# Router logits computed before the token rows are transposed, and a new order of expert steps in the first layer

## What is computed

```python
s = sigmoid(t @ w_router)                 # t: (tokens, 1024), 16 experts
sel = s + b_router
# best of 4 groups by the sum of its top 2, then the top 2 experts inside it
wts = wts / sum(wts)
for e in range(16):
    y = (silu(t @ w_gate[e]) * (t @ w_up[e])) @ w_down[e]     # 1024 -> 512 -> 1024
    out = out + combine[:, e:e + 1] * y
```

## Time and profile before

| | |
|---|---|
| median of 3 runs | 1533.33 us (1530.64 to 1534.82) |
| the profiled execution | 1535.0 us, span 1533.2 us |
| PE busy | 1305.8 us, 85% |
| DVE busy | 606.1 us, 40% |
| ACT busy | 411.2 us, 27% |
| DMA | 381.25 MB, mean 249 GB/s |
| mean granted clock of TensorE | 0.911 |

### The profile page before, as it was taken

One profiled execution on the slowest core, in us unless ns is written; L12 is line 12 of the kernel. 1 busy time (PEld: TensorE's weight loads), 2 busy tenths in 40 slices (PEclk: granted clock), 3 DMA queues, 4 the chain that ended last, 5 costly groups with the idle time before them and its releaser, 6 DMA issues.

```text
span 1533.2 us, 19883 instructions
## 1 busy us (share of the span) xinstructions
PE 1305.8 (85%) x8082; PEld 819.7 (53%) x8082; DVE 606.1 (40%) x1069; ACT 411.2 (27%) x643; POOL 117.0 (8%) x111
## 2 busy tenths in 40 slices
PE   3889999899999799899989836998799858778873
PEld 1477777687777353234333335876688634222321
DVE  0445567676462621111121145557767351101112
ACT  1432236462341400010000026336556300000000
POOL 0000000000040020000000020009702010000001
PEclk9889999999999869899999957999999959979986
DMA  9676753222220599869997953763334469999995
GB/s 385 250 285 247 288 224 150 72 77 76 90 84 6 218 347 385 328 243 366 367 390 265 374 210 140 317 258 138 115 133 141 190 264 330 393 408 387 402 422 180
DMA packets 63951, 381.25 MB, mean 249 GB/s; under 512 B 9552, under 2 KB 14356, under 8 KB 24436
## 3 DMA queue, kind: packets, MB, share of 16 engines
q1 hardware_dynamic: 45056, 338.71, 56.6%
q10 hardware_dynamic: 14708, 24.36, 4.8%
q0 software_dynamic: 4096, 16.91, 3.1%
HBM read 358.71 MB, written 42.21 MB: 261 GB/s over the span
## 4 chain that ended last, share of the span: by engine, by line
issue 42%; PE 37%; DVE 8%; ACT 5%; DMA 5%; POOL 3%; ACTq 0%; POOLq 0%; DVEq 0%; SPq 0%
PE bank L1734 9%; PE bank L1735 8%; PE bank L1736 8%; PE bank L1742 2%; POOL m_lo L645 2%; DMA hrow_d<-in_hy_bias 1%; PE bank L1700 1%; ACT L679 1%; DMA raw<-in_mod 1%; DMA stage<-in_in 1%; POOL x_rows L659 1%; DMA yg<-y_rows,rowid 1%; PE bank L1999 1%; PE bank L1750 1%; DVE wlo L1099 1%
## 5 line engine op out<-in xcount | busy, mean ns | idle before, releaser
L2085 PE MATMUL bank<-wexp,xg 128*64 128x512 f32 (+1 forms) x1504 | 294.6, 646 | 60.0 <-DMA wexp<-in_expert 57.0
L1734 PE MATMUL bank<-h_hi,whi 128*128 128x512 f32 (+1 forms) x640 | 227.8, 356 | 6.8 <-DVE h_lo L1099 5.7
L1735 PE MATMUL bank<-h_lo,whi 128*128 128x512 f32 (+1 forms) x640 | 221.3, 346 | 0.0
L1736 PE MATMUL bank<-h_hi,wlo 128*128 128x512 f32 (+1 forms) x640 | 220.8, 345 | 0.0
L2085 PEld LDWEIGHTS bank<-wexp,xg 128*64 128x64 f32 (+1 forms) x1504 | 79.2, 131 | 237.1 <-issue 160.4
L1099 DVE TENSOR_TENSOR wlo<-stage,whi 128x2048 fp32r<-128x2048 f32 x56 | 132.0, 2365 | 66.2 <-ACT whi L679 53.5
L2100 PE MATMUL bank<-wexp,act_a 128*32 128x256 f32 (+1 forms) x1072 | 146.0, 497 | 6.8 <-DVE act_a L1099 6.5
L679 ACT ACTIVATE yrow<-bank 128x512 f32<-128x512 f32 (+1 forms) x47 | 23.8, 506 | 435.7 <-PE bank L2100 346.2
L1734 PEld LDWEIGHTS bank<-h_hi,whi 128*128 128x128 f32 x640 | 125.3, 196 | 27.8 <-DVE h_lo L1099 7.9
L1735 PEld LDWEIGHTS bank<-h_lo,whi 128*128 128x128 f32 x640 | 125.5, 196 | 13.4 <-issue 0.5
L1736 PEld LDWEIGHTS bank<-h_hi,wlo 128*128 128x128 f32 x640 | 125.3, 196 | 13.7
(11 more groups left out here) (282 smaller groups left out, 1703.0 us busy)
## 6 DMA issues: line engine op xcount, KB each, us to landing
wexp<-in_expert SPq DMA_DIRECT2D x192, 1024.0 KB, 16.3
stage<-in_in SPq DMA_DIRECT2D x40, 1024.0 KB, 4.9
stage<-in_mod SPq DMA_DIRECT2D x26, 1024.0 KB, 7.2
spare<-in_mod SPq DMA_DIRECT2D x14, 1024.0 KB, 18.3
x_rows<-in_c_zero SPq DMA_DIRECT2D x20, 512.0 KB, 7.3
y_rows<-in_c_zero SPq DMA_DIRECT2D x20, 512.0 KB, 8.8
stage<-in_out SPq DMA_DIRECT2D x8, 1024.0 KB, 4.8
raw<-in_mod SPq DMA_DIRECT2D x8, 1024.0 KB, 7.1
```

The lines of the kernel that those rows point to most:

```text
L1734: MM(o, w[0], x_[0], start=start, stop=False)
L1735: MM(o, w[0], x_[1], start=False, stop=False)
L1736: return MM(o, w[1], x_[0], start=False, stop=stop)
L2085: ins = MM(bank[0][g * w:(g + 1) * w, :], x_[:, 2 * j + k, :], wexp[:, z, j, c], start=(first_ == 0), stop=(last_ == 0))
```

## The change

In both layers TensorE now makes all eight logit products first; only then come the transposes of the row banks, b = 0 first, then those of the logits, then the other banks. ScalarE loads the sigmoid's table before it makes h2T, makes all h2T tiles in one run, and copies all row banks but the last two after the sigmoid; VectorE copies the last two after its masks. Of the eight lead units two stand before "places" and six after. In layer 0 the order of ranks is another: ranks 5, 7, 4, 8, 3 and 11 come first, and the four steps of ranks 1, 0 and 2 are parted by steps of ranks 10, 12, 14, 9, 13 and 6. Capacities, layer 1's order and all arithmetic are the same.

```diff
-ORDER = ((3, 3, 4, 4, 1, 11, 1, 1, 1, 0, 10, 0, 14, 0, 13, 0, 7, 5, 5, 12, 2, 2, 6, 2, 2, 8, 9),
+ORDER = ((5, 5, 7, 4, 4, 8, 3, 3, 11, 1, 1, 10, 1, 12, 1, 0, 0, 14, 0, 9, 0, 2, 2, 13, 2, 6, 2),
          (0, 7, 9, 5, 3, 3, 14, 4, 11, 2, 2, 13, 8, 1, 1, 12, 6, 10))
...
                 pool.wait_ge(S("rowid_ok"), 1)
-                pool.wait_ge(S("row_a"), T // P)
-                pool.wait_ge(S("row_d"), T // P)
+                pool.wait_ge(S("row_a"), 2 * (T // P) - 2)
+                pool.wait_ge(S("row_d"), 2)
...
+                nc.scalar.preload_act_table(ACT.Sigmoid)
                 for k in range(KT):
                     act.wait_ge(S("hn"), (KT if l == 0 else 2 * KT) + k + 1)
...
-                    if 4 <= k < 4 + NT and k % 2 == 0:
-                        rows_out_(k - 4)
 
                 act.wait_ge(S("lg"), 1)
                 fn(lgT[:, 0:T], bank[7][0:NE, 0:T], ACT.Copy).then_inc(S("lgT"), 1)
-                rows_out_(NT)
                 act.wait_ge(S("lg"), 2)
                 fn(rt[:, 0, 0:NT * NE], bank[7][:, 0:NT * NE], ACT.Sigmoid).then_inc(S("affin"), 1)
-                for b in range(NT + 2, 2 * NT, 2):
+                for b in range(2 * NT - 2):
                     rows_out_(b)
...
-                for b in range(1, NT, 2):
-                    rows_out_(b)
...
                 ins.then_inc(S("routed"), 1)
-                for b in range(NT + 1, 2 * NT, 2):
+                for b in range(2 * NT - 2, 2 * NT):
                     rows_out_(b)
...
                     ins = MM(bank[7][0:NE, 0:T], wr[:, k, :], h2T[:, k, 0:T], start=(k == 0), stop=(k == KT - 1))
-                    if k < 4:
-                        for t in range(NT):
-                            row = T_(row_bank(t)[:, k * P:(k + 1) * P], h2T[:, k, t * P:(t + 1) * P])
-                            if k == 3:
-                                row.then_inc(S("rows"), 1)
                 ins.then_inc(S("lg"), 1)
-                for t in range(NT):
-                    if NT + t >= 7:
-
-                        pe.wait_ge(S("row_a"), 1)
+                for b in range(2 * NT):
+                    if b >= 7:
+
+                        pe.wait_ge(S("row_a"), b - 6)
                     for k in range(4):
...
                 if l < DEPTH - 1:
-                    pe.wait_ge(S("row_a"), 3)
-                    pe.wait_ge(S("row_d"), 2)
-                    lead_units(0, LEAD // 2)
+                    pe.wait_ge(S("row_a"), LEAD_BANK + 1)
+                    lead_units(0, 2)
                 pe.wait_ge(S("routed"), 1)
...
                 if l < DEPTH - 1:
-                    lead_units(LEAD // 2, LEAD)
-                pe.wait_ge(S("row_a"), NT)
-                pe.wait_ge(S("row_d"), NT)
+                    lead_units(2, LEAD)
+                pe.wait_ge(S("row_a"), 2 * NT - 2)
+                pe.wait_ge(S("row_d"), 2)
```

More of the change, by code:

```diff
@@ L1999, in _ @@
                     ins = MM(bank[7][0:NE, 0:T], wr[:, k, :], h2T[:, k, 0:T], start=(k == 0), stop=(k == KT - 1))
-                    if k < 4:
-                        for t in range(NT):
-                            row = T_(row_bank(t)[:, k * P:(k + 1) * P], h2T[:, k, t * P:(t + 1) * P])
-                            if k == 3:
-                                row.then_inc(S("rows"), 1)
                 ins.then_inc(S("lg"), 1)
-                for t in range(NT):
-                    if NT + t >= 7:
-                        pe.wait_ge(S("row_a"), 1)
+                for b in range(2 * NT):
+                    if b >= 7:
+                        pe.wait_ge(S("row_a"), b - 6)
                     for k in range(4):
-                        row = T_(row_bank(NT + t)[:, k * P:(k + 1) * P], h2T[:, 4 + k, t * P:(t + 1) * P])
+                        row = T_(row_bank(b)[:, k * P:(k + 1) * P], h2T[:, 4 * (b // NT) + k, (b % NT) * P:(b % NT + 1) * P])
                     row.then_inc(S("rows"), 1)
-                    if t == 0:
+                    if b == 0:
                         pe.wait_ge(S("lgT"), 1)
```

## The result

The changed kernel took 1517.26 us (median of four runs, 1512.96 to 1518.20), the kernel before 1534.07, measured beside it (four runs, 1530.64 to 1540.98): a ratio of 0.9872, 95% interval 0.9852 to 0.9892, so 16.8 us less. A later comparison gave 0.9895 (0.9865 to 0.9924). The forecast was 8.4 us less, with a range that reached to 1516. The direction held; the size was half of what came.

A forecast was written before the change was run, and what follows sets the result against it. Layer 0's experts were taken as bound by weights for 70 us, then mostly TensorE; layer 1's by weights. Gains of 4.8 (layer 0) and 3.6 (layer 1) sum to 8.4 us: 1533.3 to 1524.9 us, range 1516 to 1532.

The forecast's parts named there:

- What bounds the kernel: Layer 0's expert stage: weights for its first 70 us, then mostly TensorE; layer 1's expert stage: weights alone.
- The dynamic tail behind: End of layer 0's expert stage, one extra item, its weights and row stores: left as it is, no gain.
- Routing, layer 0: Layer 0's sigmoid, and the weight stream after it, come 4.6 us earlier.
- The new order: Layer 0's 27 expert steps under the new rank order end at 867.3 instead of 872.1, 4.8 us earlier.
- The 37th piece: Layer 0's weight stream: rank 1's fourth piece, counted from the restart at 554.9, lands at 674.9 and releases TensorE.
- rival (c): Better than forecast: layer 0's weights come at 3.0 us a piece and tail waits shrink; 1516 us, chance 0.15.
- Rival (a): Layer 0's order gives back the earlier stream's gain, leaving only layer 1's 3.6 us; 1529.7 us, chance 0.14.
- Rival (b): Slower: weight starvation in layer 0's steps 2 to 9 decides, slower overall from 3.42 us a piece; 1542, chance 0.08.
- stretch at half clock: Sign against the mechanism: TensorE running at half clock behind 680 us in layer 0; a 14 us stretch costs 7 us.
- Rival (d): All eight router products run at low clock, layer 0's sigmoid 0.4 us later; 1531.1 us, held in (a)'s chance.
- Routing, layer 1: Layer 1's sigmoid and its weight stream start 3.6 us earlier, all of it kept; bounds 2.4 to 5.3.
- The table load: ScalarE's sigmoid table load leaves the path to the sigmoid in each layer: 1.28 us, no drain counted.

The follow-up runs named there:

- number 3: The changed kernel with only the end of layer 0's order altered, so that single-step rank 9 again comes last in slot 0; 1522.56 us, ratio 0.9910.
- numbers 1: The changed kernel with layer 0's old order of ranks, so only the routing is new; 1526.91 us, ratio 0.9944.
- number 5: New routing and old order, with the six weight pieces of layer 0's extra item cut to 256 columns; 1517.07 us, ratio 0.9886.
- number 4: New routing with the old order's first 19 steps and its end changed to the new order's pattern; 1524.26 us, ratio 0.9933.
- number 11: The changed kernel itself, unaltered, measured once more; 1516.06 us, ratio 0.9895.
- number 7: The changed kernel without the sigmoid's table load ahead of the h2T pieces; 1516.47 us, ratio 0.9860.

## Why the prediction was right in direction and half in size

**What bounds the kernel** was read rightly for the steps and for layer 1, and stopped one stretch short. Of the rows behind 872 us I used only TensorE's small waits for weights. The step that failed is the sentence "The dynamic tail behind (one extra item, its weights and the row stores) I leave as it is". It was costed at 0 and is worth -5.4 us, the largest miss. The signs lay in the trace of before: the old order's last load into slot 0, the item's six pieces behind it in one queue, and ScalarE's waits of 7.2 and 5.6 us for row stores. What the runs showed in its place: the order alone takes 5.7 us off this stretch (344.4 to 338.7), pieces held back in the new order give 4.1 of it back, and small pieces in the old order take 8.2 off. A step that is moved takes its DMAs along, and I followed these for the head and not for the end.

**Routing, layer 0**: forecast -4.6, measured -5.3 to the sigmoid (products with the router 9.09 us; I had the low clock hold for 4 us). The forecast also slipped in its own sum: at the row's 1.03 us a product, 5.7 products take 5.9 us and not 5.6, so it should have read -4.3. To the restart of the stream it is another -0.8. What stood ahead came out 2.2 us later, in code that the change does not touch; over all profiled kernels it ranges from 504.6 to 510.8 us.

**The new order.** The 37th piece lands 117.9 us behind the restart (120.0 forecast): the first after 6.8 us (5.2), the next 18 at 3.21 us each (3.28), the next 18 at 2.95 (3.10). Step 10 to the end took 186.1 us (187.5), without a wait for weights. In parts that is +1.6, -1.2 and -2.6 us to the 37th piece and -1.4 behind it, 3.4 us between the forecast's -0.2 and the -3.6 measured. To the 37th piece that is rival (c), the faster stream, to a third: it had this piece 6.8 us earlier. How much of these 3.4 us is the order and how much the clock stays open. Summed from the clock's records between 566 and 862 us, half clock lasted 17.1 us before and 3.4 after; over the four kernels with the old head 3.4 to 21.5, over the nine with a new one 0 to 10.7. The old head takes 311.5 to 322.2 us from the restart, the new ones 308.1 to 311.8, so both ranges overlap by a little.

**Rival (a), routing alone pays**, is out: the order alone gave 11.9 us. Rival (c) had named 1516, 1.3 us from the time measured, and that is luck: it took 6.8 us from a faster stream, of which 2.1 came, and the shorter end of the stage, which made up the rest, is not in it. **Rival (b), the starved start decides**, is out too: the spacing would have had to be 3.42. No stretch at half clock stood behind 680 us before the fixed steps ended. The Trainium skill's account of a clock that falls again and again in short products beside DMA waits (TensorE: Matmul & The Clock Gate, HAM oscillation) did not come true here for the starved head: of its 123 us behind the restart, 3 (595 to 598) ran at half clock beside the stretch that lay there already. **Rival (d)** is out: the products with the router came at 9.09 us and not 15.

**Routing, layer 1**: forecast -3.6, measured -3.3. With the old routing the stretch is 10.46 and 11.36 us in two traces, with the new one and its early table load 6.15 to 7.20 in ten, so the true gain lies between 3.3 and 5.2. The weight stream starts 11.8 us behind the sigmoid on both sides, and from there to the columns of layer 1's extra item it is 257.4 and 256.9 us, so all of it stayed, as argued.

**The table load**: costed at 1.28 us in each layer; taking it back costs 0.8 to 0.9 in each by the trace, since it runs beside the small transposes, and nothing that the runs can tell.

## What to carry to other kernels

A stage's end has its own critical path: here small stores that wait for one another beside the large transfers still in flight, and a last item that waits for its weights. Where a schedule is changed, follow the last loads of each queue as far as the last store, and ask which piece stands ahead of which in the queue; here the slot of one single step at the end was worth 3.1 us (number 3 against the changed kernel, to layer 1's routing) to 5.8 (the same two by their ratios), and the whole new head some 4 by the times of numbers 1 and 3. An earlier start in front of a stream that bounds the stage was worth almost nothing: 8.3 us bought 0.8.

## What was not expected of the hardware

A row store of 128 KB took 9.7 us beside a DMA share of 1.0 (before, 874 to 890), 7.7 where the share was 1.0 only to 874 (changed kernel), and 3.3 us beside one of 0.20 (changed kernel) or 0.15 (number 5, window 872 to 880).

TensorE's clock accounts for much of the scatter of one profile against another. From 910 to 1200 us, where all these kernels run the same code, shifted by up to 20 us, the window rows of number 4 and number 11 are:

```profile
910.00:1200.00 290.00, 251.51 (x1935) 223.34 (x1935) 185.48 (x301) 145.49 (x213) 71.83 (x72) 0.91 0.45 168
```

```profile
910.00:1200.00 290.00, 250.72 (x1983) 222.25 (x1981) 181.28 (x281) 143.73 (x215) 73.21 (x72) 0.95 0.49 183
```

0.91 and 0.95 granted, by the records 53.0 and 30.7 us at half clock, and 318.0 and 311.9 us from the combining transposes to layer 1's router. A stretch's difference of a few us between two profiles is therefore read only together with its clock. And the stretch from 527 to 564 us ran at 0.50 in the changed kernel though TensorE was busy for 36.15 of its 37 us, and so did its like in all kernels but number 7, in which the same products ran at 0.99; what decides between the two I did not find.
